# The first norm of a hybrid encoder block on one core: its transposes with products of zeros between them, its row scaling in blocks on three engines

## The chip, the cores and the metric

The kernel runs on one core of a Trainium2 chip. The metric is the device time of one execution in microseconds (us). TensorE (PE in the rows; PEld are its weight loads) multiplies matrices and transposes, VectorE (DVE), ScalarE (ACT) and GpSimd (POOL) work elementwise, SyncE (SP) only issues transfers. Each engine runs its own list of instructions in order; engines meet at semaphores, which an instruction raises when it is done and another engine's list waits for. TensorE's clock has two levels in what follows, 1.2 GHz and 2.4 GHz; the view by stretches shows them as a granted clock of 0.50 and 1.00.

## The reference

```python
meta = jnp.broadcast_to(meta_tokens[None], (bsz, 16, 2048))
hs = jnp.concatenate([meta, x], axis=1)              # 272 rows of 2048
h = rms_norm(hs, norm_mix)                           # x * rsqrt(mean(x*x) + 1e-6) * g
z = h @ w_in                                         # split into u_ssm, q, k, v, gates
y_a = s5_mixer(u_ssm, ...); y_b = windowed_gqa(q, k, v, attn_sink)
merged = g[0] * (y_a @ w_proj_ssm) + g[1] * (y_b @ w_proj_attn)
hs = hs + merged @ w_out
hs = hs + peer_ffn(rms_norm(hs, norm_ffn), ...)      # 8 heads x 16 experts of 16384, per row
return rms_norm(hs, norm_final)[:, 16:]
```

All is float32. The change touches only the first two lines that compute something: the norm `h` of the 16 meta rows and the 256 rows of x, in the form in which the product with `w_in` reads it.

## The kernel before, in words

The program is one straight list per engine, with the order written by hand. Its stages are: the norm of the 272 rows and its transpose; ten tiles of weights (48 matmuls each) for u and k; two for v; eight heads of attention and the state-space scans, with the gate products between; the projections; and, from about 750 us on, 256 steps that gather one expert row for each token and multiply (L1276, L1708).

The products of the first stages are made of three matmuls each, since a float32 number is split into a high part (`hH`, `wh`) and a rest (`hL`, `low_ring`) of a narrower type: high by high, rest by high, high by rest (L1338, L1339, L1340 of `split_product`). For weight tile n, SyncE loads it into `ring`, ScalarE rounds it into `wh` (`high(n)`, L483), and VectorE subtracts to get `low_ring` (`low(n)`, L810). For tile 0 this subtraction is GpSimd's (L410), and TensorE waits for it by `s_first`.

The norm goes like this. SyncE loads the meta rows (128 KB), the two halves of x (`xn[:, 0]` and `xn[:, 1]`, 1 MB each), the parameters `prm` (620 KB) and then weight tiles. ScalarE squares and sums the meta rows (L489), the first 128 rows of x (L492) and the second 128 (L496). VectorE turns each sum into a factor in a chain of small steps: `factors` (L890), a square root on ScalarE (L494, L498), then `rstd` (L880 to L884), once for the meta rows and the first half, and once for the second half. The rows are then scaled into `xs` (which lies in `gates`): the first half by VectorE (L898), the meta rows by ScalarE (L500), the second half by VectorE (L900). After all three, TensorE transposes 16 blocks k of 128 columns: 16 meta rows (L1351) and two times 128 rows (L1353) into one of four banks of `ps`; ScalarE takes a bank out as `hH[:, k]` (L505), VectorE takes the rest `hL[:, k]` (L905). After the sixteenth `hL` TensorE begins the first weight tile (L1338). GpSimd then makes two copies for later stages, `hX` (L415, written into `xn`) and `hLx` (L416).

Of the kernel before, what the change touches and what calls it, by code (L numbers as in the profile page):

```python
# [66 lines left out]
def build(nc, W, keys, par, bw, cw, meta, x, gffn, gfin, u_tab, v_tab, out):  # L67
    top = ExitStack()
    with top:
        def sem(name):  # L70
# [25 lines left out]
        st = sbt(top, "st", [P, 16])  # L96
        halfpi = sbt(top, "halfpi", [P, 1])
# [71 lines left out]
        xs = gates[:, 0:3 * D].rearrange("p (t d) -> p t d", t=3)  # L169
        squares = [a[:, :, :].rearrange("p k t -> p (k t)") for a in (ybT, yT)]  # L170
# [65 lines left out]
        s_par = sem("s_par")  # L236
# [8 lines left out]
        s_sq, s_ms, s_sqr, s_xs = sem("s_sq"), sem("s_ms"), sem("s_sqr"), sem("s_xs")  # L245
        s_meta, s_xsm, s_gv = sem("s_meta"), sem("s_xsm"), sem("s_gv")
# [220 lines left out]
        def _(act):  # L467
            act.sem_inc(s_hT, 4)
# [20 lines left out]
            nc.scalar.activation(squares[0][0:META, :], xs[0:META, TT, :], ACT.Square, accum_out=st[0:META, 1:2]).then_inc(s_sq, 1)  # L489
            act.wait_ge(s_x[0], 16)  # L490
            act.wait_ge(s_sq, 1)
            nc.scalar.activation(squares[0], xn[:, 0, :], ACT.Square, accum_out=st[:, 0:1]).then_inc(s_sq, 1)  # L492
            act.wait_ge(s_ms, 2)
            nc.scalar.activation(st[:, 6:8], st[:, 3:5], ACT.Sqrt).then_inc(s_sqr, 1)  # L494
            act.wait_ge(s_x[1], 16)
            nc.scalar.activation(squares[1], xn[:, 1, :], ACT.Square, accum_out=st[:, 2:3]).then_inc(s_sq, 1)  # L496
            act.wait_ge(s_ms, 3)
            nc.scalar.activation(st[:, 8:9], st[:, 5:6], ACT.Sqrt).then_inc(s_sqr, 1)  # L498
            act.wait_ge(s_meta, 1)
            nc.scalar.activation(xs[0:META, TT, :], xs[0:META, TT, :], ACT.Copy, scale=st[0:META, 10:11]).then_inc(s_xsm, 1)  # L500
            high(0, back=None)

            for k in range(KT):
                act.wait_ge(s_tr, k + 1)
                nc.scalar.activation(hH[:, k, :], ps[:, k % 4, 0:L], ACT.Copy, scale=col("gmix", k, k + 1)).then_inc(s_hT, 1)  # L505
# [277 lines left out]
        def _(dve):  # L783
# [8 lines left out]
            dve.sem_inc(s_hL, 4)  # L792
# [85 lines left out]
            def rstd(dst, ss, v, root):  # L878
# [8 lines left out]
            def factors(a, b, g):

                dve.wait_ge(s_sq, 2 + g)
                nc.vector.tensor_scalar(st[:, 3 + a:3 + b], st[:, a:b], 1.0 / D, EPS, ALU.mult, ALU.add).then_inc(s_ms, 1)  # L890
                dve.wait_ge(s_ms, 2 + g)
                dve.wait_ge(s_sqr, 1 + g)
                rstd(st[:, 9 + a:9 + b], st[:, a:b], st[:, 3 + a:3 + b], st[:, 6 + a:6 + b])
# [421 lines left out]
        def _(pe):  # L1315
# [39 lines left out]
            pe.wait_ge(s_hL, 4 + KT)
# [449 lines left out]
```

## Time and profile before

| | us |
|---|---|
| median of 3 runs | 2074.19 (2071.4 to 2074.27) |
| the profiled execution, its own time | 2074.33 |
| its span, first to last instruction | 2072.5 |
| TensorE busy | 1767.6 (85%) |
| VectorE busy | 1281.2 (62%) |
| GpSimd busy | 797.3 (38%) |
| ScalarE busy | 468.9 (23%) |
| from the start to the first transpose | 14.17 |
| from the start to the first matmul of weight tile 0 | 28.66 |

The busy times overlap, so they don't add to the span. What a change in one stage is worth is read from the waits of that stage. The profiled execution lies 0.14 us above the median, and 1.8 us of it lie outside the span.

### The profile page before, as it was taken

The page shows a single profiled execution, that of the slowest core. Times are in us where ns is not written, and L with a number is a line of the kernel's source. Part 1 is how long each engine was busy: PE and PEld are TensorE (multiplying, and loading weights), DVE is VectorE, ACT ScalarE, POOL GpSimd, SP SyncE. Part 2 cuts the span into 40 slices and gives each one's busy share as a digit, 9 for nine tenths or more (in the row PEclk, how much of TensorE's full clock was granted, in tenths as well). Part 3 has the DMA queues.
Part 4 walks back from the last instruction along what each step waited for, and adds up shares of the span by engine and source line. Part 5 has one row for each costly group of instructions (what it writes and reads, how often), then busy time and mean ns, then how long its engine had stood idle before and what let it go on. Part 6 is the DMA issues. An engine that isn't in the chain of part 4 may idle for free.

```text
span 2072.5 us, 24784 instructions
## 1 busy us (share of the span) xinstructions
PE 1767.6 (85%) x8224; PEld 1109.5 (54%) x8224; DVE 1281.2 (62%) x2427; ACT 468.9 (23%) x999; POOL 797.3 (38%) x711
## 2 busy tenths in 40 slices
PE   7999999998999999879879977777777777777776
PEld 5988888887998865435425532223222322222222
DVE  4535987783555365666567666666666575666654
ACT  5334655654434311001011010001000000010001
POOL 2022233330350044445455454444453553543432
PEclk9999999999999999999999999999999999999999
DMA  5488799997455589999999999999999999999997
GB/s 191 157 186 202 167 210 213 209 211 210 175 184 183 211 339 421 421 422 422 422 422 422 420 423 421 422 421 413 421 421 403 406 420 389 422 412 422 422 422 294
DMA packets 115893, 692.89 MB, mean 334 GB/s; under 512 B 12880, under 2 KB 12880, under 8 KB 41168
## 3 DMA queue, kind: packets, MB, share of 16 engines
q0 software_dynamic: 96768, 599.83, 76.8%
q1 hardware_dynamic: 19040, 92.00, 12.5%
q8 instruction: 45, 0.74, 0.1%
q14 instruction: 40, 0.33, 0.0%
HBM read 689.68 MB, written 2.10 MB: 334 GB/s over the span
## 4 chain that ended last, share of the span: by engine, by line
PE 47%; DMA 33%; issue 8%; DVE 7%; POOL 3%; ACT 1%; DVEq 0%; POOLq 0%; SPq 0%; ACTq 0%
DMA uv<-u_tab,eid 31%; PE ps L1708 14%; PE ps L1658 3%; PE ps L1421 3%; PE ps L1426 3%; PE ps L1338 2%; PE ps L1339 2%; PE ps L1340 2%; PE ps L1428 2%; PE ps L1427 2%; PE ps L1530 2%; POOL uv L463 2%; DVE uv L1276 2%; PE ps L1641 1%; PE ps L1640 1%
## 5 line engine op out<-in xcount | busy, mean ns | idle before, releaser
L1708 PE MATMUL ps<-uv,dg 128*128 128x512 f32 x2048 | 962.6, 616 | 263.4 <-DVE dg L1282 251.2
L1708 PEld LDWEIGHTS ps<-uv,dg 128*128 128x128 f32 x2048 | 381.7, 194 | 821.7 <-issue 480.5
L1276 DVE CUSTOM_DVE_ANT_0 uv<-uv,xn 128x2048 f32<-128x2048 f32 x256 | 587.2, 2294 | 378.4 <-DMA uv<-u_tab,eid 360.0
L463 POOL DMA_INDIRECT uv<-v_tab,eid x256 | 288.2, 1126 | 598.7 <-PE ps L1708 346.4
L460 POOL DMA_INDIRECT uv<-u_tab,eid x256 | 332.3, 1298 | 199.5 <-issue 184.1
L756 ACT ACTIVATE ga<-av 128x1 f32<-128x1 f32 x256 | 51.9, 203 | 1185.1 <-DVE av L1276 1185.1
L810 DVE TENSOR_TENSOR low_ring<-ring,wh 128x2048 fp32r<-128x2048 f32 x43 | 99.9, 2328 | 77.7 <-ACT wh L483 77.6
L1426 PE MATMUL ps<-hH,parts 128*128 128x256 f32 x480 | 146.1, 304 | 0.4 <-DMA parts<-W 0.4
L1427 PE MATMUL ps<-hLx,parts 128*128 128x256 f32 x480 | 134.6, 280 | 0.0
L1428 PE MATMUL ps<-hH,parts 128*128 128x256 f32 x480 | 134.5, 280 | 0.0
L1282 DVE TENSOR_SCALAR dg<-prm,ga,gw 128x128 f32<-128x128 f32 x256 | 92.9, 363 | 66.7 <-ACT ga L756 32.6
L433 POOL DMA_DIRECT2D parts<-W x80 | 70.5, 881 | 158.8 <-ACT parts L595 124.3
L429 POOL DMA_DIRECT2D parts<-W x80 | 47.1, 588 | 174.8 <-PE ps L1428 106.1
L483 ACT ACTIVATE wh<-ring 128x2048 fp32r<-128x2048 f32 x44 | 84.3, 1916 | 131.3 <-PE ps L1340 98.7
L1658 PE MATMUL ps<-h2T,ring 128*128 128x256 f32 x448 | 100.8, 379 | 0.0
L1658 PEld LDWEIGHTS ps<-h2T,ring 128*128 128x128 f32 x448 | 85.0, 190 | 21.8 <-issue 11.5
L1426 PEld LDWEIGHTS ps<-hH,parts 128*128 128x128 f32 x480 | 90.2, 188 | 6.8 <-issue 5.0
L1427 PEld LDWEIGHTS ps<-hLx,parts 128*128 128x128 f32 x480 | 90.4, 188 | 1.0
L1428 PEld LDWEIGHTS ps<-hH,parts 128*128 128x128 f32 x480 | 90.4, 188 | 0.0
L1421 PE MATMUL ps<-xn,ring 128*128 128x256 f32 x320 | 76.6, 382 | 0.0
L595 ACT ACTIVATE parts<-parts 128x768 fp32r<-128x768 f32 x60 | 50.4, 841 | 102.4 <-DMA parts<-W 102.4
L1421 PEld LDWEIGHTS ps<-xn,ring 128*128 128x128 f32 x320 | 57.9, 190 | 7.7 <-issue 0.7
(282 smaller groups left out, 2300.8 us busy)
## 6 DMA issues: line engine op xcount, KB each, us to landing
ring<-W SPq DMA_DIRECT2D x64, 1024.0 KB, 4.9
parts<-W POOLq DMA_DIRECT2D x160, 384.0 KB, 5.7
ring<-W SPq DMA_DIRECT2D x40, 256.0 KB, 5.3
xn<-x SPq DMA_DIRECT2D x4, 1024.0 KB, 10.7
uv<-u_tab,eid POOLq DMA_INDIRECT x256
uv<-v_tab,eid POOLq DMA_INDIRECT x256
bwt<-bw SPq DMA_DIRECT2D x8, 256.0 KB, 5.9
cwt<-cw SPq DMA_DIRECT2D x8, 256.0 KB, 6.2
```

The costliest lines, as they stand in the source:

```text
L460: pool.indirect_dma_start(uv[:, s, 0, :], None, u_tab, at).then_inc(s_u[s], 16)
L463: pool.indirect_dma_start(uv[:, s, 1, :], None, v_tab, at).then_inc(s_vv[s], 16)
L483: nc.scalar.activation(high_slot(n), ring[:, n % RING, :], ACT.Copy).then_inc(s_high, 1)
L810: nc.vector.tensor_tensor(low_ring[:, n % RING, :], ring[:, n % RING, :], high_slot(n), ALU.subtract).then_inc(s_low, 1)
L1276: nc.vector.tensor_tensor_reduce(uv[:, j % UV, 0, :], uv[:, j % UV, 0, :], xn[:, T, :], 1.0, 0.0, ALU.mult, ALU.add, av[:, hh, j:j + 1]).t ...
L1282: nc.vector.tensor_scalar(dg[:, j % 2, :], ident, ga[:, hh, j:j + 1], gw[:, hh, j:j + 1], ALU.mult, ALU.mult).then_inc(s_dg, 1)
L1421: nc.tensor.matmul(dst, whole(t)[:, k, :], hX[:, k, :], start=(k == 0), stop=False)
L1426: nc.tensor.matmul(dst, wh[:, m, :], hH[:, k, META:L], start=False, stop=False)
L1427: nc.tensor.matmul(dst, wh[:, m, :], hLx[:, k, :], start=False, stop=False)
L1428: ins = nc.tensor.matmul(dst, wl[:, m, :], hH[:, k, META:L], start=False, stop=(k == 2 * PART - 1))
L1658: ins = nc.tensor.matmul(ps[:, 4 + q % 2, 0:SEQ], w[:, k, :], h2T[:, k, :], start=(k == 0), stop=(k == KT - 1))
L1708: ins = nc.tensor.matmul(ps[:, 4 * T + n, :], dg[:, j % 2, :], uv[:, j % UV, 1, n * 512:(n + 1) * 512], start=False, stop=last and i == 2 ...
```

## The change

1. Two new kinds of matmul whose operands are zeros (`warm`, 512 columns of `trig`, zeroed by VectorE's first instruction) and whose result nobody reads (bank 7 of `ps`): seven of 512 columns before the wait for the parameters, and one of 256 columns behind each of the 16 groups of transposes.
2. The transposes use six banks instead of four (`k % 6`), and the counts of `s_hT` and `s_hL` begin at 6.
3. The second half's sum of squares is shared: ScalarE takes columns 0 to 1023, VectorE columns 1024 to 2047 with a fused multiply and add (into `sums`). All three factors then come from one chain of small steps, behind the last sum.
4. The scaling is cut in blocks c of 512 columns: VectorE scales the first half, ScalarE the second (blocks 0 and 1 before its first eviction, 2 and 3 ahead of its evictions k = 2 and 4), GpSimd the meta rows. TensorE waits, ahead of group k, only for block k // 4 of each.
5. `wh` of tile 0 is no longer rounded by ScalarE but loaded by a converting transfer that GpSimd issues once the second half of x has landed. GpSimd's subtraction for tile 0 now comes behind its four scalings and that transfer.
6. GpSimd's `hX` and `hLx` wait for VectorE's fourth `low` instead of the last `hL`.

The core of the diff:

```diff
 pool:
-            pool.wait_ge(s_high, 1)
+            pool.wait_ge(s_x[TT - 1], 16)
+            pool.dma_start(high_slot(0), W[0, :, :]).then_inc(s_hd, 16)
+            pool.wait_ge(s_root, 1)
+            for c in range(4):
+                pool.tensor_scalar(xs[0:META, TT, c * 512:(c + 1) * 512], xs[0:META, TT, c * 512:(c + 1) * 512], st[0:META, 11:12], None, ALU.mult
+                                   ).then_inc(s_xs[TT], 1)
+            pool.wait_ge(s_hd, 16)
+            pool.wait_ge(s_w[0], 16)
             pool.tensor_tensor(low_ring[:, 0, :], ring[:, 0, :], high_slot(0), ALU.subtract).then_inc(s_first, 1)
-            pool.wait_ge(s_hL, 4 + KT)
-            pool.wait_ge(s_xs, TT)
-            pool.wait_ge(s_sq, 3)
+            pool.wait_ge(s_low, 4)
 scalar:
+            act.wait_ge(s_x[1], 16)
+            nc.scalar.activation(squares[1][:, 0:D // 2], xn[:, 1, 0:D // 2], ACT.Square, accum_out=st[:, 1:2]).then_inc(s_sq, 1)
             act.wait_ge(s_ms, 2)
-            nc.scalar.activation(st[:, 6:8], st[:, 3:5], ACT.Sqrt).then_inc(s_sqr, 1)
-            act.wait_ge(s_x[1], 16)
-            nc.scalar.activation(squares[1], xn[:, 1, :], ACT.Square, accum_out=st[:, 2:3]).then_inc(s_sq, 1)
-            act.wait_ge(s_ms, 3)
-            nc.scalar.activation(st[:, 8:9], st[:, 5:6], ACT.Sqrt).then_inc(s_sqr, 1)
-            act.wait_ge(s_meta, 1)
-            nc.scalar.activation(xs[0:META, TT, :], xs[0:META, TT, :], ACT.Copy, scale=st[0:META, 10:11]).then_inc(s_xsm, 1)
-            high(0, back=None)
+            nc.scalar.activation(st[:, 6:9], st[:, 3:6], ACT.Sqrt, scale=1.0 / D).then_inc(s_sqr, 1)
+            act.wait_ge(s_root, 1)
+            scaled(0)
+            scaled(1)
             for k in range(KT):
                 act.wait_ge(s_tr, k + 1)
-                nc.scalar.activation(hH[:, k, :], ps[:, k % 4, 0:L], ACT.Copy, scale=col("gmix", k, k + 1)).then_inc(s_hT, 1)
+                if k in (2, 4):
+                    scaled(1 + k // 2)
+                nc.scalar.activation(hH[:, k, :], ps[:, k % 6, 0:L], ACT.Copy, scale=col("gmix", k, k + 1)).then_inc(s_hT, 1)
 vector:
+            nc.vector.memset(warm, 0.0).then_inc(s_warm, 1)
...
-            factors(0, 2, 0)
-            dve.sem_inc(s_meta, 1)
-            nc.vector.tensor_scalar(xs[:, 0, :], xn[:, 0, :], st[:, 9:10], None, ALU.mult).then_inc(s_xs, 1)
-            factors(2, 3, 1)
-            nc.vector.tensor_scalar(xs[:, 1, :], xn[:, 1, :], st[:, 11:12], None, ALU.mult).then_inc(s_xs, 1)
+            dve.wait_ge(s_x[1], 16)
+            nc.vector.tensor_tensor_reduce(squares[1][:, D // 2:], xn[:, 1, D // 2:], xn[:, 1, D // 2:], 1.0, 0.0,
+                                           ALU.mult, ALU.add, sums[:, 1:2]).then_inc(s_half, 1)
+            dve.wait_ge(s_half, 1)
+            dve.wait_ge(s_sq, 1 + TT)
+            nc.vector.scalar_tensor_tensor(st[:, 3:6], st[:, 0:3], D * EPS, sums[:, :], ALU.add, ALU.add).then_inc(s_ms, 1)
+            rstd(st[:, 9:12], st[:, 0:3], st[:, 3:6], st[:, 6:9], 1.0 / D)
+            dve.sem_inc(s_root, 1)
+            for c in range(4):
+                nc.vector.tensor_scalar(xs[:, 0, c * 512:(c + 1) * 512], xn[:, 0, c * 512:(c + 1) * 512], st[:, 9:10], None, ALU.mult
+                                        ).then_inc(s_xs[0], 1)
 tensor:
+            pe.wait_ge(s_warm, 1)
+            for _ in range(7):
+                nc.tensor.matmul(ps[:, 7, :], warm[:, 0:P], warm, start=True, stop=True)
             pe.wait_ge(s_par, 16)
-            pe.wait_ge(s_xs, TT)
-            pe.wait_ge(s_xsm, 1)
             for k in range(KT):
+                for t in range(TT + 1):
+                    pe.wait_ge(s_xs[t], k // 4 + 1)
...
                 ins.then_inc(s_tr, 1)
+                nc.tensor.matmul(ps[:, 7, 0:256], warm[:, 0:P], warm[:, 0:256], start=True, stop=True)
-            pe.wait_ge(s_hL, 4 + KT)
+            pe.wait_ge(s_hL, 6 + KT)
```

TensorE's list at the program's start, before: group after group of three transposes (`prm` holds the identity, `gates` the scaled rows), then tile 0.

```order
L1314 UNCONDITIONAL_BRANCH [waits barrier_Pool_Activation_PE_DVE_SP_release]
L1351 MATMUL ps<-prm,gates 128x16 [waits s_hT,s_xsm,s_hL,s_xs,s_par]
L1353 MATMUL ps<-prm,gates 128x128 x2
L1351 MATMUL ps<-prm,gates 128x16 [waits s_hL,s_hT]
...
L1338 MATMUL ps<-hH,wh 128x272 [waits s_uk,s_first,s_hL]
```

And now, where `trig` holds the zeros:

```order
L1330 UNCONDITIONAL_BRANCH [waits barrier_Pool_Activation_PE_DVE_SP_release]
L1362 MATMUL ps<-trig 128x512 [waits s_warm]
L1362 MATMUL ps<-trig 128x512 x6
L1371 MATMUL ps<-prm,gates 128x16 [waits s_xs2,s_hT,s_xs1,s_hL,s_xs0,s_par]
L1373 MATMUL ps<-prm,gates 128x128 x2
L1375 MATMUL ps<-trig 128x256
L1371 MATMUL ps<-prm,gates 128x16 [waits s_hT,s_xs2,s_hL,s_xs1,s_xs0]
```

The transposes keep their order; seven products stand ahead of them, and one between each group and the next. The wait of tile 0 is the same.

GpSimd's list at the program's start, before:

```order
L405 UNCONDITIONAL_BRANCH [waits barrier_Pool_Activation_PE_DVE_SP_gather]
L410 ISA
L410 TENSOR_TENSOR low_ring<-ring,wh 128x2048 [waits s_high]
L415 TENSOR_TENSOR xn<-hH,hL 128x1024 [waits s_sq,s_xs,s_hL]
L416 COPY hLx<-hL 128x3072
```

And now (`gates` are the meta rows of `xs`, `st` their factor):

```order
L408 UNCONDITIONAL_BRANCH [waits barrier_Pool_Activation_PE_DVE_SP_gather]
L413 DMA wh<-W 128x2048 [waits s_x1]
L416 ISA
L416 TENSOR_SCALAR gates<-gates,st 16x512 [waits s_root]
L416 TENSOR_SCALAR gates<-gates,st 16x512 x3
L420 TENSOR_TENSOR low_ring<-ring,wh 128x2048 [waits s_w0,s_hd]
L423 TENSOR_TENSOR xn<-hH,hL 128x1024 [waits s_low]
```

A transfer and four scalings now stand ahead of the subtraction for tile 0, and a setup instruction (`ISA`) that stood at the head of the list stands behind a wait for x.

## Rows read from the trace of the kernel before

**Rows 1.** Time line of the start: start us, length us, engine, line, operation [idle before].
```profile
8.22 0.19 ACT L492 ACTIVATION_READ_ACCUMULATOR ybT<-xn 128x1 f32 x1
8.52 0.17 DVE L890 TENSOR_SCALAR st<-st 128x2 f32<-128x2 f32 x1 [6.35 <-ACT ybT L492]
8.90 1.91 ACT L496 ACTIVATE yT<-xn 128x2048 f32<-128x2048 f32 x1
10.13 1.28 DVE L898 TENSOR_SCALAR gates<-xn,st 128x2048 f32<-128x2048 f32 x1
12.79 1.28 DVE L900 TENSOR_SCALAR gates<-xn,st 128x2048 f32<-128x2048 f32 x1
14.17 0.25 PE L1351 MATMUL ps<-prm,gates 16*128 16x16 f32 x1 [14.17 <-DVE gates L900]
...
26.64 0.28 PE L1351 MATMUL ps<-prm,gates 16*128 16x16 f32 x1
...
28.10 0.50 DVE L905 SCALAR_TENSOR_TENSOR hL<-ps,prm,hH 128x272 fp32r<-128x272 f32 x1 [0.33 <-ACT hH L505]
...
28.66 0.59 PE L1338 MATMUL ps<-hH,wh 128*128 128x272 f32 x1 [1.11 <-DVE hL L905]
...
32.22 0.35 PE L1338 MATMUL ps<-hH,wh 128*128 128x272 f32 x1
32.42 0.29 PE L1339 MATMUL ps<-hL,wh 128*128 128x272 f32 x1
32.54 0.29 PE L1340 MATMUL ps<-hH,low_ring 128*128 128x272 f32 x1
```
**Rows 2.** View of the tile xn, 0 to 30 us: issue to landing of its two transfers.
```profile
DMA to landing us min/median/max: 5.2/6.2/7.2
```
**Rows 3.** Waits from 28 to 130 us: engine, what waited, for whom; total, times, longest.
```profile
POOL parts L429 <- PE ps L1340: 55.9, 1, 55.9
ACT wh L483 <- PE ps L1340: 40.1, 10, 6.8
```
**Rows 4.** Busy time by stretches: TensorE, its weight loads, VectorE, ScalarE, GpSimd, granted clock, DMA.
```profile
14.00:28.50 14.50, 13.37 (x48) 7.44 (x48) 7.98 (x17) 9.53 (x18) 4.53 (x1) 1.00 0.38 157
35.00:72.00 37.00, 37.00 (x300) 37.00 (x299) 20.92 (x42) 13.19 (x12) 0.83 (x1) 1.00 0.49 171
244.00:247.40 3.40, 1.36 (x12) 1.15 (x10) 3.33 (x12) 3.36 (x9) 1.26 (x3) 1.00 0.23 67
247.40:254.20 6.80, 5.90 (x73) 5.05 (x73) 6.43 (x17) 2.64 (x9) 1.61 (x3) 0.50 0.95 184
254.20:258.00 3.80, 3.80 (x27) 3.59 (x26) 3.80 (x11) 3.77 (x9) 0.87 (x1) 1.00 0.56 124
```
**Rows 5.** Time line of TensorE elsewhere: transposes and float32 products (two records each).
```profile
108.21 1.89 PE L1421 MATMUL ps<-xn,ring 128*128 128x256 f32 x8
...
248.30 0.70 PE L1530 MATMUL ps<-uP,bwH 32*128 32x136 f32 x4 [2.94 <-DVE pb L1074]
...
251.64 1.12 PE L1465 MATMUL ps<-prm,hs 128*128 128x128 f32 x4
...
715.82 1.09 PE L1626 MATMUL ps<-prm,hs 128*128 128x128 f32 x8 [1.38 <-DVE hs L1194]
```
**Rows 6.** Groups of instructions by line: busy us, mean ns of one, idle before.
```profile
L1276 DVE CUSTOM_DVE_ANT_0 uv<-uv,xn 128x2048 f32<-128x2048 f32 x256 | 587.2, 2294 | 378.4 <-DMA uv<-u_tab,eid 360.0
...
L505 ACT ACTIVATE hH<-ps,prm 128x272 fp32r<-128x272 f32 x16 | 7.8, 486 | 5.0 <-PE ps L1353 4.8
```
**Rows 7.** Groups of GpSimd by line and shape.
```profile
L446 POOL TENSOR_TENSOR mL<-fresh,mH 128x256 f32 x16 | 38.9, 2430 | 13.1 <-ACT mH L688 13.1
L444 POOL TENSOR_TENSOR fresh<-bwt 128x256 f32<-128x256 f32 x16 | 11.8, 740 | 80.3 <-DVE bwt L1181 80.3
...
L410 POOL TENSOR_TENSOR low_ring<-ring,wh 128x2048 fp32r<-128x2048 f32 x1 | 4.5, 4525 | 15.0 <-ACT wh L483 15.0
```
**Rows 8.** DMA issues of the page: KB each, us from issue to landing.
```profile
parts<-W POOLq DMA_DIRECT2D x160, 384.0 KB, 5.7
```
**Rows 9.** Line L810, VectorE's subtraction: shortest, median, longest ns.
```profile
L810 DVE TENSOR_TENSOR low_ring<-ring,wh x43: 2278/2293/3306, 29.9 to 700.5; 128x2048 fp32r<-128x2048 f32 x43
```

More of the change, by code:

```diff
@@ L96, in build @@
         st = sbt(top, "st", [P, 16])
+        sums = sbt(top, "sums", [P, 3])
         halfpi = sbt(top, "halfpi", [P, 1])
@@ L169, in build @@
         xs = gates[:, 0:3 * D].rearrange("p (t d) -> p t d", t=3)
+        warm = trig[:, :, :, :, :].rearrange("p a b u t -> p (a b u t)")[:, 0:512]
         squares = [a[:, :, :].rearrange("p k t -> p (k t)") for a in (ybT, yT)]
@@ L231, in nth_low @@
             return n - 1 if n < W_Q else W_Q - 1 + n - W_PROJ
-        s_par = sem("s_par")
+        s_par, s_warm, s_half, s_hd = sem("s_par"), sem("s_warm"), sem("s_half"), sem("s_hd")
+        s_root = sem("s_root")
         s_x = [sem(f"s_x{t}") for t in range(TT + 1)]
@@ L244, in build @@
         s_trig0, s_f0 = sem("s_trig0"), sem("s_f0")
-        s_sq, s_ms, s_sqr, s_xs = sem("s_sq"), sem("s_ms"), sem("s_sqr"), sem("s_xs")
-        s_meta, s_xsm, s_gv = sem("s_meta"), sem("s_xsm"), sem("s_gv")
+        s_sq, s_ms, s_sqr, s_xs = sem("s_sq"), sem("s_ms"), sem("s_sqr"), [sem(f"s_xs{t}") for t in range(TT + 1)]
+        s_gv = sem("s_gv")
         s_hT, s_hL = sem("s_hT"), sem("s_hL")
@@ L467, in _ @@
         def _(act):
-            act.sem_inc(s_hT, 4)
+            act.sem_inc(s_hT, 6)
+            act.sem_inc(s_high, 1)
             act.sem_inc(s_uk, 2)
@@ L488, in _, with scaled @@
             act.wait_ge(s_x[TT], 16)
[L489 removed]
+            nc.scalar.activation(squares[0][0:META, :], xs[0:META, TT, :], ACT.Square, accum_out=st[0:META, 2:3]).then_inc(s_sq, 1)
+            act.wait_ge(s_sq, 1)
             act.wait_ge(s_x[0], 16)
[L491 removed]
             nc.scalar.activation(squares[0], xn[:, 0, :], ACT.Square, accum_out=st[:, 0:1]).then_inc(s_sq, 1)
+            act.wait_ge(s_x[1], 16)
+            nc.scalar.activation(squares[1][:, 0:D // 2], xn[:, 1, 0:D // 2], ACT.Square, accum_out=st[:, 1:2]).then_inc(s_sq, 1)
             act.wait_ge(s_ms, 2)
[L494 to L501 removed]
+            nc.scalar.activation(st[:, 6:9], st[:, 3:6], ACT.Sqrt, scale=1.0 / D).then_inc(s_sqr, 1)
+            act.wait_ge(s_root, 1)
+            def scaled(c):
+                nc.scalar.activation(xs[:, 1, c * 512:(c + 1) * 512], xn[:, 1, c * 512:(c + 1) * 512], ACT.Copy, scale=st[:, 10:11]
+                                     ).then_inc(s_xs[1], 1)
+            scaled(0)
+            scaled(1)
+            act.wait_ge(s_par, 16)
             for k in range(KT):
                 act.wait_ge(s_tr, k + 1)
[L505 removed]
+                if k in (2, 4):
+                    scaled(1 + k // 2)
+                nc.scalar.activation(hH[:, k, :], ps[:, k % 6, 0:L], ACT.Copy, scale=col("gmix", k, k + 1)).then_inc(s_hT, 1)
             high(1)
@@ L791, in _ @@
             dve.sem_inc(s_pm, 2)
-            dve.sem_inc(s_hL, 4)
+            dve.sem_inc(s_hL, 6)
             dve.sem_inc(s_hs, 4)
@@ L876, in discretise, with rstd @@
                 yield step(ins)
-            def rstd(dst, ss, v, root):
+            def rstd(dst, ss, v, root, unit=1.0):
                 step(nc.vector.reciprocal(dst, root))
@@ L882, in rstd @@
                 step(nc.vector.tensor_tensor(ss, ss, v, ALU.mult))
-                step(nc.vector.tensor_scalar(ss, ss, -0.5, 1.5, ALU.mult, ALU.add))
+                step(nc.vector.tensor_scalar(ss, ss, -0.5 * unit, 1.5, ALU.mult, ALU.add))
                 step(nc.vector.tensor_tensor(dst, dst, ss, ALU.mult))
[L887 to L893, printed above, removed]
@@ L1350, in _ @@
                 c = slice(k * P, (k + 1) * P)
-                nc.tensor.transpose(ps[:, k % 4, 0:META], xs[0:META, TT, c], ident[0:META, 0:META])
+                nc.tensor.transpose(ps[:, k % 6, 0:META], xs[0:META, TT, c], ident[0:META, 0:META])
                 for t in range(TT):
-                    ins = nc.tensor.transpose(ps[:, k % 4, META + t * P:META + (t + 1) * P], xs[:, t, c], ident)
+                    ins = nc.tensor.transpose(ps[:, k % 6, META + t * P:META + (t + 1) * P], xs[:, t, c], ident)
                 ins.then_inc(s_tr, 1)
-            pe.wait_ge(s_hL, 4 + KT)
+                nc.tensor.matmul(ps[:, 7, 0:256], warm[:, 0:P], warm[:, 0:256], start=True, stop=True)
+            pe.wait_ge(s_hL, 6 + KT)
             for m in range(W_V):
```

7 lines of the change are left out of this document (5 added, 2 removed).

## The prediction

> **What bounds the kernel now.** I read the time line of the start first, then the waits behind it, then the stretches. In the time line [rows 1] the reader is to see three pieces in series. The norm's factors and scalings take until 14.17 us, where TensorE starts its first transpose, held by the last scaling L900. Sixteen groups of transposes take until 26.64 us for the last group's start, 12.47 us or 0.831 us a group. The tail of evictions takes 2.02 us more, and at 28.66 us tile 0 begins. All before 28.66 is a serial head, and no product of the program overlaps it. Behind it TensorE does not rest: 37.00 of 37.00 us between 35 and 72 us [rows 4]. The other engines wait for TensorE there, ScalarE's rounding 40.1 us in ten waits and GpSimd's first transfer of `parts` 55.9 us [rows 3]. So what follows the head is released by TensorE's own progress, not by a fixed time, and a head that is x us shorter moves everything by x. I found nothing that gives it back.
>
> The clock is the second thing in [rows 1]. The matmuls of 272 columns from 28.66 to 32.22 us follow each other at about 0.226 us (15 intervals less the first's late start), those after 32.42 at 0.12. The first is the 1.2 GHz level, the second the 2.4 GHz level, though the stretches' clock column says 1.00 for both. TensorE had been "busy" 13.37 of 14.5 us with transposes before [rows 4] without the clock rising; it rose after 3.5 us of back-to-back products. The 16 slow matmuls cost 3.56 us from 28.66 to 32.22, where 16 at 0.124 would take 1.98: 1.6 us that a full clock gives back. The transposes are at the slow level as well: four of them at granted 0.50 take 1.12 us, eight at 1.00 take 1.09 [rows 5], so 0.23 against 0.117 us each.
>
> **The change part by part.**
>
> The factors. The second half of x lands at 8.9 us: its square begins at 8.90 [rows 1], and the later of the two transfers takes 7.2 us [rows 2]. Before, ScalarE then squares 2048 columns (1.91 us, 0.19 to read the sum). Now it squares 1024: half of 1.91 plus about 0.1 of fixed cost, 1.05, plus 0.19, ends at 10.15. VectorE's half is of the kind of L1276, a product summed along the row, 2.29 us for 2048 [rows 6], so 1.2 us for 1024 and it ends at 10.1. From the end of a sum (8.41) to the first scaling (10.13) the small steps take 1.72 us [rows 1]; the chain is the same length for three columns. So all factors are known at 11.87, against 12.79 for the last before.
>
> The scaling. VectorE's block of 512 is a quarter of 1.28, some 0.4 us. ScalarE's is as its eviction of 272 (0.486 us [rows 6]) with 240 columns more, 0.6 to 0.7. GpSimd's block of 16x512 is not in the trace: from below 0.74 us (L444, half as many columns, 128 rows), from above 2.43 us (L446) [rows 7]. The rate of L410, 4.5 us for 2048 with two inputs, gives 1.13 for 512, and I take 1.2. GpSimd's is then the last to be ready, at 11.9 + 1.3 = 13.2 us (12.7 to 14.4), so transposes start 1.0 us earlier. Blocks 1 to 3 are ready long before groups 4, 8 and 12, at 1.2 us a block against 3.4 us for four groups, and even at 2.43.
>
> In the trace VectorE's subtraction took 3.31 us beside GpSimd's L415 against a median of 2.29 [rows 9], so the two slow each other. The Trainium skill, page "SBUF — State Buffer", section "Who interferes with whom", says why: a pair of SBUF ports is shared by the two engines and locked for a whole instruction, also by VectorE's scalings of float32 in their fast mode. By it GpSimd's first block may wait for VectorE's, some 0.4 us more; without it the first transpose is at 13.2, with it at 13.6. The trace agrees that there is a conflict, and not with which instruction.
>
> The transposes with products between. At 2.4 GHz three transposes take 3 x 0.117 = 0.35 us, a float32 product of 256 columns 0.43 (eight records, 1.89 us less a tail of 0.17, for four products) [rows 5]. What else is in a group of before is 0.831 - 0.21 - 2 x 0.23 = 0.16 us at the slow clock; I take half of it, 0.08. Sum 0.86 us a group, bounds 0.78 (nothing of it) and 0.94 (all). Fifteen groups take 12.9 us against 12.47: the products take back what the doubled clock gives. ScalarE needs 16 x 0.49 + 2 x 0.65 = 9.1 us of it and VectorE 8.0, both less than 13.8, so TensorE sets the pace and the six banks bring nothing. The tail shrinks from 2.02 to 1.65, since the last three transposes take 0.35 and not 0.7; the last product runs beside the evictions.
>
> Tile 0 so begins at 13.2 + 12.9 + 1.65 = 27.75 us, 0.9 earlier, and at full clock, 1.6 more. Sum: 2.5 us.
>
> Tile 0's weights. ScalarE loses 1.9 us of rounding and 2.0 of meta scaling, which both lay ahead of its evictions. GpSimd now has the issue of the transfer (8.9), four blocks to 16.7, and then the subtraction, 4.5 us. The transfer of 1 MB that converts is not in the trace. Those of 384 KB land 5.7 us after issue [rows 8]: from below 5.7, from above in proportion 15.2, and my value is 8, since much of the 5.7 is fixed. It lands at 17 to 18, so the subtraction ends at 22.5 and is hidden by 5 us; at the upper bound (24.5 + 4.5 = 29.0) it is not. Moving `hX` and `hLx` behind the fourth `low` puts 7 us of GpSimd work at about 48 to 55 us; it may slow one or two of VectorE's `low` by 1 us, of which a tile of 6 us holds one (1.9 + 2.3 us of work), so nothing; the copies are read only from 108.2 us on [rows 5]. VectorE's first `low` is no longer slowed, and was hidden.
>
> The seven products ahead cost nothing in themselves unless they end after 13.2. They begin at about 2.4 us. A product of 512 columns is 0.86 us at full clock and 1.73 at half; seven take 6.0 or 12.1 us. If the clock rises after 3.5 us of them, as it did in tile 0, they end at 10.2; if later, at up to 11.5; if never, at 14.5, which costs 1.3 us.
>
> **The rivals.** Everything hangs on the clock at 13.2 us. TensorE is then idle for 1.7 to 3.0 us.
>
> A, the forecast: the clock stays up through gap and groups. 2074.33 - 2.5 = 2071.8 by the profiled execution, 2071.7 by the median (0.14 less).
>
> B: it falls in the gap and comes back during the groups. For it: 2.94 us of rest before 248.30 ended with a clock of 0.50 for 6.8 us [rows 4, 5]; against it: the rest before 715.82, 1.38 us, did not. The slow stretch there lasted 6.8 us, four groups at 1.69, and I allow for half of it. Two to four groups at 0.83 + 0.86 = 1.69 us instead of 0.86 cost 1.7 to 3.3 us: 2073.4 to 2075.0.
>
> C, the other side: it falls in the gap and the groups do not bring it back. The place is TensorE's groups, and it decides when transposes with products at the slow clock are no more to it than transposes alone, which had 13 us and did not raise it [rows 4]. Fifteen groups at 1.69 are 25.4 us, tile 0 begins at 13.2 + 25.4 + 2.0 = 40.6 us and at the slow clock: 12 us more, 2086. Against it: with four transposes in it the stretch of 247.4 to 254.2 us was followed by full clock [rows 4, 5]. In the Trainium skill, page "TensorE: Matmul & The Clock Gate", Part 4, transposes are said not to count as work for the clock gate. By that rule the zeros alone hold or raise it, half of the engine's time; the trace agrees in that 13 us of transposes raised nothing. That is C's mechanism, and it makes a fall in the gap dearer.
>
> D: GpSimd becomes late with tile 0, by the upper bound of the transfer or by blocks of 2.43 us. Tile 0 begins at 29 to 30 us, 0.3 to 1.3 later than before; with 1.6 from the clock that is 2073 to 2074, and the wait may cost the clock too.
>
> E: all goes at the lower bounds, start at 12.7 and 0.78 us a group: tile 0 at 12.7 + 11.7 + 1.6 = 26.0, with 1.6 from the clock 4.3 us, 2069.9.
>
> **How the numbers follow.** A 0.38, B 0.24, C 0.18, D 0.10, E 0.10. The predicted time is A's, 2071.7. A's own range is 2069.7 to 2073.7, from the bounds of start and group. The runs of before spread by 2.9 us, and clock dips in the expert stage shift with the start. The whole range goes from 2067.5 to 2081 and leaves out C. Faster or slower is told from 0.2%, 4.1 us. Faster by more needs E or the lower edge of A: 0.22. Slower is C and a little of D: 0.20. The rest, 0.58, is within.
>
> **What would show it.** Right: the second half's scaling begins near 11.9 us, the first transpose near 13.2, groups follow at 0.86 us, tile 0 begins near 27.7 with matmuls at 0.124 us from the first. Wrong: groups at 1.7 us or transposes of 0.23 us each (B, C), a tile 0 that waits for GpSimd's subtraction (D), a first transpose much later than 14, or a gain in the head that a wait before 250 us gives back.

## The result and the profile after

| | before | changed |
|---|---|---|
| median of 17 runs, us | 2073.63 | 2080.45 |
| profiled execution, its own time, us | 2074.33 | 2079.42 |
| its span, us | 2072.5 | 2077.6 |

The ratio is 1.0033, 95% interval 1.0026 to 1.0039: the change makes the kernel 6.8 us slower. The forecast was 2071.7 us, 2.5 us faster. Two of the seventeen runs of the changed kernel took 3071 and 3536 us; their cause is open, the ratio leaves them out, and without them its median is 2080.24. The time lies at the edge of the range given (2081), but on the side to which 0.20 was allotted. That it lies inside is luck: no rival of the prediction has a time between 2075.0 us, the upper end of B, and C's 2086, and C's mechanism, which costs 12 us, did not occur.

The time line of the changed kernel's start answers to [rows 1] (start us, length us, engine, line, operation, and the rest ahead of it in brackets; the seven products are 14 records):

```profile
2.49 7.92 PE L1362 MATMUL ps<-trig 128*128 128x512 f32 x14 [2.49 <-DVE trig L817]
...
4.36 0.34 PEld L1362 LDWEIGHTS ps<-trig 128*128 128x128 f32 x1 [0.52 <-issue]
5.21 0.34 PEld L1362 LDWEIGHTS ps<-trig 128*128 128x128 f32 x1 [0.52 <-issue]
5.95 0.19 PEld L1362 LDWEIGHTS ps<-trig 128*128 128x128 f32 x1 [0.40 <-issue]
6.38 0.19 PEld L1362 LDWEIGHTS ps<-trig 128*128 128x128 f32 x1 [0.24 <-issue]
...
8.99 0.71 POOL L413 DMA_DIRECT2D wh<-W  x1 [8.53 <-DMA xn<-x]
...
11.67 1.34 ACT L509 ACTIVATE gates<-xn,st 128x512 f32<-128x512 f32 x2 [1.16 <-DVEq L913]
11.72 2.37 DVE L915 TENSOR_SCALAR gates<-xn,st 128x512 f32<-128x512 f32 x4
11.74 6.85 POOL L416 TENSOR_SCALAR gates<-gates,st 16x512 f32<-16x512 f32 x4 [2.04 <-DVEq L913]
...
14.18 0.26 PE L1371 MATMUL ps<-prm,gates 16*128 16x16 f32 x1 [3.77 <-DVE gates L915]
...
15.84 0.28 PE L1371 MATMUL ps<-prm,gates 16*128 16x16 f32 x1
...
17.52 0.28 PE L1371 MATMUL ps<-prm,gates 16*128 16x16 f32 x1
...
19.01 4.52 POOL L420 TENSOR_TENSOR low_ring<-ring,wh 128x2048 fp32r<-128x2048 f32 x1 [0.42 <-DMA wh<-W]
...
19.21 0.28 PE L1371 MATMUL ps<-prm,gates 16*128 16x16 f32 x1
...
20.24 0.23 PE L1371 MATMUL ps<-prm,gates 16*128 16x16 f32 x1
...
21.20 0.23 PE L1371 MATMUL ps<-prm,gates 16*128 16x16 f32 x1
...
30.82 0.23 PE L1371 MATMUL ps<-prm,gates 16*128 16x16 f32 x1
...
32.53 0.39 PE L1354 MATMUL ps<-hH,wh 128*128 128x272 f32 x1 [0.68 <-DVE hL L921]
```

Three things are to be read here. The factors are ready at 11.7 us, 1.1 us earlier than the second chain before, but the first transpose is at 14.18 us, as before. The row names VectorE's scalings (L915), of which TensorE waits only for the first; GpSimd's first block took 2.07 us, the longest of its four, and ended at 13.8. The 0.37 us from there to the transpose has no cause that the rows show. The first three groups follow at 1.68 us and the others at 0.96. And tile 0 begins at 32.53 us, 3.87 later than in [rows 1], though at 0.123 us a matmul from its second on.

The clock, in the view by stretches (busy us of TensorE, weight loads, VectorE, ScalarE, GpSimd; granted clock; DMA):

```profile
5.80:12.60 6.80, 4.61 (x11) 1.71 (x9) 3.10 (x10) 4.30 (x7) 1.57 (x2) 1.00 1.01 421
12.60:19.40 6.80, 5.22 (x16) 3.17 (x16) 2.50 (x5) 2.31 (x5) 6.38 (x5) 0.50 1.03 420
19.40:32.50 13.10, 12.45 (x65) 7.72 (x64) 6.92 (x14) 7.55 (x16) 4.14 (x1) 1.00 0.20 81
```

The products ahead raised it: their weight loads follow at 0.85 us up to 5.21 and at 0.43 from 5.95 on. (The column alone doesn't tell this, since it says 1.00 for the slow transposes of before as well.) It fell within TensorE's rest of 3.77 us (the whole rest lies between 10.4 and 14.18) and came back during the groups. This is the mechanism of rival B; B's own time was 2073.4 to 2075.0, so more was lost than that.

Behind the head there is one more loss, with a cause that can be seen. The time line from 55 to 64 us:

```profile
55.17 5.33 DVE L842 TENSOR_TENSOR gates<-gates 128x64 f32<-128x64 f32 x3
55.33 2.39 POOL L423 TENSOR_TENSOR xn<-hH,hL 128x1024 f32<-128x1024 f32 x1 [31.79 <-DVE low_ring L826]
...
57.67 2.75 POOL L424 CAST hLx<-hL 128x3072 fp32r<-128x3072 f32 x1
...
60.53 0.23 DVE L844 TENSOR_TENSOR gates<-prm,gates 128x64 f32<-128x64 f32 x1
...
61.25 2.29 DVE L826 TENSOR_TENSOR low_ring<-ring,wh 128x2048 fp32r<-128x2048 f32 x1
...
63.59 0.39 PE L1354 MATMUL ps<-hH,wh 128*128 128x272 f32 x1 [0.77 <-DVE low_ring L826]
```

The view of line L842 has the three apart (ns: shortest, median, longest):

```profile
L842 DVE TENSOR_TENSOR gates<-gates x3: 218/2386/2656, 55.2 to 57.8; 128x64 f32<-128x64 f32 x3
```

Two of VectorE's three small steps take 2.39 and 2.66 us, each about as long as the copy of GpSimd's beside it (2.39 and 2.75), where the third takes 0.22 and the next step of the same size, L844, 0.23. So `low` of tile 5 starts late, and TensorE rests 0.77 us, with a gap of 1.05 us in its tiles. The Trainium skill, page "SBUF — State Buffer", section "Who interferes with whom", says that a VectorE instruction with two SBUF inputs contends with a GpSimd instruction that reads SBUF, and that the port pair that they share is an exclusive lock. The trace agrees: each of the two steps (L842 has two inputs) is held for one whole copy.

And there is one without a visible cause. ScalarE's roundings, one a tile, show TensorE's pace. Before:

```profile
42.66 1.92 ACT L483 ACTIVATE wh<-ring 128x2048 fp32r<-128x2048 f32 x1 [3.77 <-PE ps L1340]
48.63 1.92 ACT L483 ACTIVATE wh<-ring 128x2048 fp32r<-128x2048 f32 x1 [3.78 <-PE ps L1340]
54.60 1.92 ACT L483 ACTIVATE wh<-ring 128x2048 fp32r<-128x2048 f32 x1 [3.77 <-PE ps L1340]
```

After:

```profile
44.92 1.92 ACT L492 ACTIVATE wh<-ring 128x2048 fp32r<-128x2048 f32 x1 [3.82 <-PE ps L1356]
50.94 1.91 ACT L492 ACTIVATE wh<-ring 128x2048 fp32r<-128x2048 f32 x1 [3.82 <-PE ps L1356]
56.94 1.92 ACT L492 ACTIVATE wh<-ring 128x2048 fp32r<-128x2048 f32 x1 [3.80 <-PE ps L1356]
```

A tile takes 5.97 us before and 6.01 after, though its 48 matmuls are the same.

### The profile page after: what moved, and what is told of

Its sections match the earlier page's. It is cut to its first block, busy times and chain, and to the rows that moved or that the text cites. A ratio compares the mean times of both kernels' runs of the same rounds, so it can differ in the third digit from the quotient of the medians.

```text
span 2077.6 us, 24900 instructions
## 1 busy us (share of the span) xinstructions
PE 1777.0 (86%) x8270; PEld 1115.7 (54%) x8270; DVE 1286.1 (62%) x2427; ACT 467.1 (22%) x1000; POOL 796.7 (38%) x716
## 4 chain that ended last, share of the span: by engine, by line
PE 46%; DMA 34%; issue 8%; DVE 7%; POOL 3%; ACT 1%; DVEq 0%; POOLq 0%; SPq 0%; ACTq 0%
DMA uv<-u_tab,eid 32%; PE ps L1729 14%; PE ps L1442 3%; PE ps L1679 3%; PE ps L1447 3%; PE ps L1449 2%; PE ps L1448 2%; PE ps L1551 2%; POOL uv L471 2%; DVE uv L1292 2%; PE ps L1354 2%; PE ps L1355 2%; PE ps L1356 2%; DMA parts<-W 2%; PE ps L1663 1%
## 5 line engine op out<-in xcount | busy, mean ns | idle before, releaser
L471 POOL DMA_INDIRECT uv<-v_tab,eid x256 | 270.7, 1058 | 601.8 <-PE ps L1729 342.2
L468 POOL DMA_INDIRECT uv<-u_tab,eid x256 | 344.5, 1346 | 201.7 <-issue 185.2
L1298 DVE TENSOR_SCALAR dg<-prm,ga,gw 128x128 f32<-128x128 f32 x256 | 93.4, 365 | 67.1 <-ACT ga L770 32.6
L1679 PEld LDWEIGHTS ps<-h2T,ring 128*128 128x128 f32 x448 | 85.2, 190 | 21.6 <-issue 11.5
## 6 DMA issues: line engine op xcount, KB each, us to landing
uv<-v_tab,eid POOLq DMA_INDIRECT x256, 14.4
```

What stands on the lines that cost most here:

```text
L468: pool.indirect_dma_start(uv[:, s, 0, :], None, u_tab, at).then_inc(s_u[s], 16)
L471: pool.indirect_dma_start(uv[:, s, 1, :], None, v_tab, at).then_inc(s_vv[s], 16)
L1298: nc.vector.tensor_scalar(dg[:, j % 2, :], ident, ga[:, hh, j:j + 1], gw[:, hh, j:j + 1], ALU.mult, ALU.mult).then_inc(s_dg, 1)
L1679: ins = nc.tensor.matmul(ps[:, 4 + q % 2, 0:SEQ], w[:, k, :], h2T[:, k, :], start=(k == 0), stop=(k == KT - 1))
```

## The experiments

All ratios are to the kernel before, run on the same chip.

**The products of zeros, alone and together.** Four kernels on one chip.

```diff
# nomid: without the products between
-                nc.tensor.matmul(ps[:, 7, 0:256], warm[:, 0:P], warm[:, 0:256], start=True, stop=True)
# nolead: without the seven ahead
-            pe.wait_ge(s_warm, 1)
-            for _ in range(7):
-                nc.tensor.matmul(ps[:, 7, :], warm[:, 0:P], warm, start=True, stop=True)
# nozeros: without both
# lead11: eleven ahead
-            for _ in range(7):
+            for _ in range(11):
```

> The changed kernel without the sixteen products of zeros between the groups of transposes; the seven ahead stay. Theory 1 (the products between cost more than the clock they keep): groups follow at about 0.83 us at the slow clock as before the change, tile 0 begins at 14.2 + 12.5 + 2.0 = 28.7 us instead of 32.5, but its first matmuls are at 0.226 us for some 3.5 us (1.6 us lost), so about 2.2 us less than the changed kernel. Theory 2 (the five waits of a group cost the time, not the products): groups at 0.95 us or more also without them, tile 0 not before 30.5 us. In both the stall of tile 5 behind GpSimd's copies stays, so the kernel stays slower than the one before.

> The changed kernel without the seven products of zeros ahead; those between the groups stay. Theory 1 (groups with a product raise the clock by themselves): the first three to six groups at 1.68 us, the others at 0.96, tile 0 begins between 32.5 and 36 us, total within 0 to 3 us of the changed kernel. Rival C of the prediction (transposes with products at the slow clock don't raise it): all groups at 1.68 us, tile 0 at 14.2 + 25.2 + 2 = 41.4 us and slow at first, total 10 us above the changed kernel.

> The changed kernel without any product of zeros. Theory 1: as without the sixteen between, tile 0 at about 28.7 us with the slow clock for its first 3.5 us, total 2.2 us below the changed kernel; the difference to that variant tells what the seven ahead are worth by themselves (expected nothing, or up to 1 us if some of the first groups run fast). What then is left against the kernel before is the scaling, the waits and GpSimd's copies: some 1 us slower than before or more.

> The changed kernel with eleven products of zeros ahead instead of seven, to fill TensorE's rest from 10.4 to 14.2 us. Theory 1 (the rest makes the clock fall and costs 2.2 us in three groups of 1.68 us): no group at 1.68, all at 0.96, tile 0 at 14.4 + 14.4 + 1.6 = 30.4 us, total 2 us below the changed kernel. Rival (the clock falls all the same, since a transpose with a product is too little work): no gain, or up to 1 us more where the eleven end after 14.2.

| kernel | tile 0 begins, us | median, us | ratio, 95% interval |
|---|---|---|---|
| changed | 32.53 | 2080.45 (other runs) | 1.0033 (1.0026 to 1.0039) |
| nomid | 28.97, slow at first | 2079.18 | 1.0022 (1.0013 to 1.0031) |
| nolead | 31.68 | 2081.64 | 1.0034 (1.0022 to 1.0047) |
| nozeros | 28.68, slow at first | 2078.96 | 1.0021 (1.0012 to 1.0030) |
| lead11 | 30.60 | 2078.50 | 1.0019 (1.0009 to 1.0029) |

The heads came out as theory 1 had them, to 0.3 us, with `nolead` 0.8 us better than its range: the groups with products raise the clock by themselves after two, and rival C is refuted. The total of `nozeros` was to be 1 us or more above before and is 4.4. In `lead11` no group is at the slow clock:

```profile
14.45 0.23 PE L1371 MATMUL ps<-prm,gates 16*128 16x16 f32 x1
14.62 0.44 PE L1373 MATMUL ps<-prm,gates 128*128 128x128 f32 x2
14.89 0.60 PE L1375 MATMUL ps<-trig 128*128 128x256 f32 x2
15.42 0.23 PE L1371 MATMUL ps<-prm,gates 16*128 16x16 f32 x1
```

Even so a group costs 0.96 us, more than the 0.83 of before at the slow clock. The totals are what opened the question anew: `nozeros` has the head of before to 0.02 us, a rest at tile 5 worth 1.05 us, and still is 0.21% slower, some 4.4 us. Some 3 us were in neither the head nor the copies.

**Where the tiles lie.** What all variants share and the kernel before lacks is the slower tile and the new tile `sums`, 12 bytes a row, declared ahead of most others. `shift12` adds that tile to the kernel before and nothing else; `sums16` widens it to 64 bytes in the changed kernel, whose instructions still use only its first three columns.

```diff
# shift12, on the kernel before
         st = sbt(top, "st", [P, 16])
+        sbt(top, "sums", [P, 3])
# sums16, on the changed kernel
-        sums = sbt(top, "sums", [P, 3])
+        sums = sbt(top, "sums", [P, 16])
```

> The kernel before with one unused tile of three columns (12 bytes a row) declared behind st, as the change adds it; no instruction differs, only the places of the tiles behind it. Theory (place of the tiles): weight tiles 0 to 9 repeat at 6.01 us as in every variant with the new tile, instead of 5.97, the stretch from the first gated merge (L1181) to the output product (L1640) takes 0.6 us more, the whole 2 to 3 us more than before. Rival (the slower pace comes from the instructions or from the chip): 5.97 us, and no difference.

> The changed kernel with the new tile widened from 3 to 16 columns (64 bytes a row). Theory (place of the tiles): weight tiles repeat at 5.97 us again and the whole is 2 to 3 us less than the changed kernel, 2077.5 to 2078.5 us. Rival: no difference, 6.01 us.

`shift12`: 2077.26 us, ratio 1.0012 (1.0004 to 1.0021). `sums16`: 2075.76 us, ratio 1.0009 (1.0000 to 1.0018), against 1.0033 with 12 bytes. The total of `sums16` is lower than expected (2077.5 to 2078.5), and not all of the difference to the changed kernel is the tile's: in its trace the clock outlasted a rest of 3.95 us and fell only in the second group, so that tile 0 begins at 31.72 us, 0.8 earlier:

```profile
14.12 0.20 PE L1371 MATMUL ps<-prm,gates 16*128 16x16 f32 x1 [3.95 <-DVE gates L915]
...
15.05 0.23 PE L1371 MATMUL ps<-prm,gates 16*128 16x16 f32 x1
...
16.37 0.28 PE L1371 MATMUL ps<-prm,gates 16*128 16x16 f32 x1
```

The weight tiles follow as the theory says. Rounding rows of `shift12`:

```profile
43.06 1.92 ACT L484 ACTIVATE wh<-ring 128x2048 fp32r<-128x2048 f32 x1 [3.80 <-PE ps L1341]
49.07 1.92 ACT L484 ACTIVATE wh<-ring 128x2048 fp32r<-128x2048 f32 x1 [3.82 <-PE ps L1341]
```

And of `sums16`:

```profile
44.07 1.92 ACT L492 ACTIVATE wh<-ring 128x2048 fp32r<-128x2048 f32 x1 [3.77 <-PE ps L1356]
50.04 1.92 ACT L492 ACTIVATE wh<-ring 128x2048 fp32r<-128x2048 f32 x1 [3.77 <-PE ps L1356]
```

6.01 us from rounding to rounding with 12 bytes and 5.97 with 64, whichever kernel it is in.

Three more tell which boundary counts. They are `shift12` with 1, 8 and 16 columns.

> The kernel before with one unused tile of one column (4 bytes a row) declared behind st. If any offset that is no multiple of 32 bytes is bad, weight tiles repeat at 6.01 us and the total rises by 2 to 3 us as with 12 bytes. If it is the distance to a 16-byte or 64-byte boundary that counts, and 12 bytes happen to be a bad place, 5.97 us and no difference.

> The same with eight columns (32 bytes a row). If the tiles' start modulo 32 bytes decides: 5.97 us a weight tile, 84.9 us from L1181 to L1640, and the time of before. If modulo 64 bytes decides: 6.01 us and 1 to 3 us more.

> The same with sixteen columns (64 bytes a row). By both rules the pace of before, 5.97 us a tile; the variants of the changed kernel with this tile took 84.3 us from L1181 to L1640 against 84.9 before, so perhaps 0.5 to 1 us less than before.

| bytes a row added to the kernel before | median, us | before beside it | ratio, 95% interval | us a weight tile |
|---|---|---|---|---|
| 4 | 2077.57 | 2073.73 | 1.0020 (1.0011 to 1.0029) | 6.01 |
| 12 | 2077.26 | 2074.71 | 1.0012 (1.0004 to 1.0021) | 6.01 |
| 32 | 2077.99 | 2073.73 | 1.0019 (1.0009 to 1.0030) | 6.01 |
| 64 | 2073.84 | 2073.73 | 1.0002 (0.9992 to 1.0011) | 5.97 |

Of the four shifts only the one of 64 bytes leaves pace and time as they were, as if the place modulo 64 bytes counted; other remainders were not run, and which of the many tiles behind it matters was not isolated. Rounding rows with 64 bytes:

```profile
43.01 1.92 ACT L484 ACTIVATE wh<-ring 128x2048 fp32r<-128x2048 f32 x1 [3.77 <-PE ps L1341]
48.98 1.92 ACT L484 ACTIVATE wh<-ring 128x2048 fp32r<-128x2048 f32 x1 [3.78 <-PE ps L1341]
```

Whether 4 and 12 bytes really move the tiles by 4 and 12, or are rounded up to 32 by the allocator, these runs don't tell. The pace explains 0.4 us in ten weight tiles, and 0.6 us between the first merge (L1181) and the output product; the rest of the 2.5 to 4.3 us was not located, since single traces differ by stretches at the slow clock (64 matmuls of L1687 take 7.41 us in the traces of `shift4` and `shift64`, 9.04 in those of `shift12` and `shift32`).

**The copies, and what is left.** `copies` puts GpSimd's two copies back behind the last hL; `trim` has that, no zeros and the 64 byte tile.

```diff
# copies
-            pool.wait_ge(s_low, 4)
+            pool.wait_ge(s_hL, 6 + KT)
```

> The changed kernel with GpSimd's two copies (hX, hLx) behind the last hL again, as before the change. Theory (the moved copies slow VectorE's subtraction for tile 5): the rest of 0.8 us ahead of tile 5 goes (the one of tile 8 stays), tiles 0 to 9 together 1.05 us shorter, total 1 us less than the changed kernel. Rival: the copies only slow another subtraction, same total.

> The changed kernel without any product of zeros, with the copies where they were before and the new tile of 16 columns: what is left is the shared sum, the scaling in blocks, six banks, and tile 0's rounding by transfer. By the theories together: first transpose at 14.2 us, groups at 0.83, tile 0 at 28.7 us and slow for 3.5 us as before the change, no rest at tile 5, tiles at 5.97 us: the time of the kernel before within 1 us (2073.5 to 2075.5). Rival: something else in the change costs 2 to 4 us, and it stays at 2077 or more.

`copies`: 2078.60 us, ratio 1.0021 (1.0013 to 1.0030); the rest ahead of tile 5 is gone and the one of tile 8 stays. The two copies now run from 32.6 to 39.8 us and lengthen `low` of tile 1 to 3.35 us, which hides. Its tiles 0 to 9 end 1.0 us earlier against their start than in the changed kernel; the medians of the two differ by 1.8 us in two sets of runs, so the size is the trace's. `trim`: 2074.16 us, ratio 0.9997 (0.9988 to 1.0006), tile 0 at 28.63 us. So the shared sum, the scaling in blocks, six banks and the transfer together neither cost nor give anything that can be told from noise (1.2 us slower to 2.5 faster): the loss is in the zeros, the copies and the place of the tiles.

**The pace of a group.** `fewaits` is `sums16` with the waits for blocks only where they can bind.

```diff
-                for t in range(TT + 1):
+                for t in range(TT + 1 if k % 4 == 0 else 0):
                     pe.wait_ge(s_xs[t], k // 4 + 1)
```

> The changed kernel with the new tile of 16 columns, and TensorE's three waits for scaled blocks only ahead of groups 0, 4, 8 and 12, where they can bind, instead of ahead of all sixteen. It is run for the groups' pace. Theory W (the satisfied waits cost TensorE's list its time): groups at the fast clock follow at about 0.86 us instead of 0.96, tile 0 begins 1.2 us earlier. Theory D (the gap lies in the switch between operands of 16 rows and of 128): 0.96 us still.

Groups at the fast clock still follow at 0.96 us (ratio 1.0007, 0.9997 to 1.0017), so the satisfied waits cost nothing. The gap comes with the group itself; whether the switch from 16 rows to 128 makes it, as theory D has it, was not isolated.

**A faster version.** If transposes alone could run at the fast clock, the products between would be needless. `c1` is `trim` with eleven products ahead. `c2` takes the scaling from GpSimd as well, has nine ahead and the waits of `fewaits`; `c2mid` is `c2` with the products between.

```diff
# c2 and c2mid; GpSimd's scalings and its wait for s_root are gone
-                nc.scalar.activation(xs[:, 1, c * 512:(c + 1) * 512], xn[:, 1, c * 512:(c + 1) * 512], ACT.Copy, scale=st[:, 10:11]
-                                     ).then_inc(s_xs[1], 1)
+                nc.scalar.activation(xs[0:META, TT, c * 512:(c + 1) * 512], xs[0:META, TT, c * 512:(c + 1) * 512], ACT.Copy,
+                                     scale=st[0:META, 11:12]).then_inc(s_xs[TT], 1)
...
+                nc.vector.tensor_scalar(xs[:, 1, c * 512:(c + 1) * 512], xn[:, 1, c * 512:(c + 1) * 512], st[:, 10:11], None, ALU.mult
+                                        ).then_inc(s_xs[1], 1)
```

> Without the products between the groups, with eleven ahead, the copies where they were, the new tile of 16 columns. Theory 1 (transposes alone cannot hold the clock, but it falls only after some of them): the first 6 to 12 groups at about 0.5 us (VectorE's and ScalarE's 0.5 us an eviction set the pace), the rest at 0.83; tile 0 between 24 and 27 us with its first matmuls slow, total 1 to 3 us less than the kernel before. Theory 2 (transposes hold it no more than rest does): it falls with the first groups, tile 0 at 28.9 us, total as before.

> As the variant with eleven ahead and none between, but VectorE scales both halves of x block by block, ScalarE the meta rows, GpSimd nothing; nine products ahead, and waits for blocks only ahead of groups 0, 4, 8, 12. Theory (GpSimd beside VectorE makes the first block late: 2.1 us for it, and 0.6 us for VectorE's instead of 0.35): first transpose at 12.5 to 12.9 us instead of 14.2, tile 0 1.3 us or more earlier than with eleven ahead, total 2 to 4 us below the kernel before. Rival: blocks of VectorE (eight) now hold groups or evictions, first transpose before 13 but tile 0 no earlier.

> The same with the sixteen products of 256 columns between the groups back. By theory 1 the clock stays up throughout, groups at 0.86 to 0.96 us, tile 0 at 12.7 + 15 x 0.91 + 1.7 = 28.0 us at the fast clock from the start: 2 us below the kernel before, and above the variant without them by up to 1 us. If the products are worth their time, it is the faster of the two instead.

| kernel | first transpose, us | a group, us | tile 0 begins, us | median, us | ratio, 95% interval |
|---|---|---|---|---|---|
| c1 | 15.12 | 0.53 | 24.78 | 2067.13 | 0.9966 (0.9953 to 0.9978) |
| c2 | 13.15 | 0.53 | 23.62 | 2068.02 | 0.9971 (0.9959 to 0.9983) |
| c2mid | 12.77 | 0.96 | 28.91 | 2071.76 | 0.9988 (0.9979 to 0.9997) |

The before beside them took 2074.45 us. `c1` and `c2` beat both kernels, the one before by 6 to 7 us and the changed one by some 13 us. They cannot be told apart from each other. Both gained more than was expected (1 to 3 and 2 to 4 us). Of the 7 us of `c1` its trace shows only 4.0: the profiled execution, 2070.26 us, is the slowest of its six, and where the others gain 3 us more is not shown. In both it is the products ahead and no scaling that hold the first transpose:

```profile
2.49 12.69 PE L1362 MATMUL ps<-trig 128*128 128x512 f32 x22 [2.49 <-DVE trig L817]
...
2.49 10.73 PE L1360 MATMUL ps<-trig 128*128 128x512 f32 x18 [2.49 <-DVE trig L813]
```

The first row is of `c1`, the second of `c2`; their weight loads halve their distance only at 8.6 and 8.3 us, while in the changed kernel and in `c2mid`, where the same products begin at the same time, they do at 5.95 and 5.8. So how long the products take differs by more than 1 us from one execution to another, and their number can't be fitted closely to the wait.

All sixteen groups of `c1` run at the fast clock (stretches; columns as above, the clock behind GpSimd's):

```profile
8.20:15.00 6.80, 6.80 (x16) 2.66 (x14) 4.60 (x12) 2.81 (x7) 3.95 (x3) 1.00 1.03 426
15.00:23.60 8.60, 8.60 (x49) 5.35 (x48) 6.08 (x14) 7.59 (x17) 8.12 (x4) 1.00 0.82 335
...
25.30:28.60 3.30, 3.30 (x18) 3.30 (x18) 2.58 (x1) 0.69 (x1) 3.30 (x2) 0.55 0.00 0
```

It falls only at about 25.6 us, 0.8 us into tile 0 and after a rest of 1.1 us between the last transpose and tile 0; tile 0's matmuls are then slow for 3.4 us, nearly the 3.6 that the kernel before pays. Whether the rest alone brought the fall, or the transposes ahead of it had a part, is not shown: a rest of 1.38 us elsewhere [rows 5] left the clock up. One half of the theory was wrong: I had it fall among the groups. `c2` and `c2mid` show that GpSimd was what held the first block: without it ScalarE's and VectorE's first blocks are ready by 12.7 us, and `c2mid`, whose nine products end at 12.0, begins at 12.77. The groups of `c2` end 2.0 us ahead of those of `c1`, but its tile 0 is only 1.2 us earlier, since a new wait takes over, GpSimd's subtraction for tile 0, which began when the transfer landed:

```profile
19.00 4.52 POOL L416 TENSOR_TENSOR low_ring<-ring,wh 128x2048 fp32r<-128x2048 f32 x1 [9.27 <-DMA wh<-W]
...
23.59 0.19 PEld L1352 LDWEIGHTS ps<-hH,wh 128*128 128x128 f32 x1 [2.13 <-DVE hL L919]
23.62 0.36 PE L1352 MATMUL ps<-hH,wh 128*128 128x272 f32 x1 [1.92 <-DVE hL L919]
```

The row names hL, which was done at 22.8; the subtraction ended at 23.52. This is rival D's place, in a kernel whose head is short enough. `c2mid` against `c2` prices the products between directly: 3.7 us by the medians, 5.3 us in tile 0's start less 1.6 for its slow matmuls. That is far more than the 1 us at most that was expected.

## Why the prediction was wrong

Right was the reading of the kernel: the head is serial, and its length passes on to the end (3.9 and 5.0 us at tile 0 in the traces of `c1` and `c2` are 4.0 and 5.5 at the end). Right to 0.2 us were the landing of x, the chain of factors (11.7 for 11.87), the seven products' end (10.4 for 10.2 to 11.5), and the 1.6 us that the fast clock gives to tile 0. The transfer landed after 10.0 us where I took 8, within its bounds, and hid as said.

The step that failed first is "Moving `hX` and `hLx` behind the fourth `low` ... so nothing". I counted 1 us for a slowed `low`; the conflict falls on the small steps of `discretise` between them, two of which then take 2.4 and 2.7 us instead of 0.2, as long as the copies. It costs 1.05 us.

Second, the clock. I gave A the greatest chance against my own rows: a rest of 2.94 us had ended with a fallen clock, the forecast gap was up to 3.0 us, and the gap came to 3.77. B was the likelier case. It costs three groups at 1.68 us instead of 0.96, 2.2 us, as B had it; `lead11` gains 1.93 us in tile 0's start by filling the gap. The trace of `sums16` has nearly the same gap (3.95) and loses 0.8 us less to the clock, so this term differs from one execution to another.

Third, the sizes within A. "I take half of it, 0.08": a group takes 0.96 us, above the upper bound of 0.94. What before was 0.16 us a group does not shrink with the clock; without a product it is 0.53 - 0.35 = 0.18. Fifteen groups take 1.5 us more than forecast. And the first transpose, 13.2 forecast within 12.7 to 14.4, came at 14.18: GpSimd's first block took 2.07 us where I took 1.2, and VectorE's four took 2.37 instead of 1.28. GpSimd's shortest block, with no scaling of VectorE's beside it, took 1.55. So 0.35 us is a block dearer than taken, and 0.5 us is, by these rows, what VectorE beside it costs; the prediction valued that lock at 0.4 us and left it out of the sum.

Fourth, and the largest single term, was in no rival: the new tile, 2.5 to 4.3 us by the three `shift` kernels that don't keep to 64 bytes, against 0.1 for the one that does. "The change part by part" priced the instructions and not the declaration.

The sum then closes within its bounds. The head is 3.87 us later, less 1.6 for its clock, so 2.3; the copies 1.05; the place of the tiles 2.5 to 4.3. Together 5.8 to 7.6 us, against 6.8 measured. In the traces alone, where the changed kernel is 5.1 us longer, 4.4 are located: 2.3, 1.05, and 1.0 of pace (0.4 and 0.6). The kernels with 64 bytes fit less well: the terms of head and copies give `fewaits` 3.4 us above before, and it measured 1.5 (0.6 below to 3.5 above).

## What to carry to other kernels

Price a declaration too: before timing a change that adds a tile, keep the bytes that it adds ahead of the other tiles a multiple of 64, or the comparison measures the shift too (putting the new tile last should do as well, but was not run). A clock that work has raised is spent on what follows, so fill the rest ahead of a short stage to its end and leave the stage itself alone; products between its steps cost more than the clock they hold. An engine brought in to help can hold the very block that is waited for, as GpSimd did here beside VectorE, and work moved "out of the way" must be checked against the small instructions that it lands beside, not only the long ones.

## What was not expected of the hardware

Transposes alone did not raise the clock in 12.5 us in the kernel before, but sixteen groups of them, 8.5 us, ran at 2.4 GHz where products had raised it first, with TensorE back to back. The Trainium skill, page "TensorE: Matmul & The Clock Gate", Part 4, says that transposes don't count as work for the gate; read by it, the clock of `c1` would have fallen among its groups. The trace shows otherwise for holding the clock over these 8.5 us, and agrees for raising it; that the clock fell 0.8 us into tile 0 leaves open how long transposes alone would hold it. The same groups at 1.2 GHz take 0.83 us and at 2.4 GHz 0.53, not half, since some 0.17 us at each group's start don't shrink (0.16 before).
